# All experts computed in one dense loop over pairs of key and value chunks, in place of gathering each token's rows

## The reference

```python
def peer(h, w_query, sub_keys, expert_u, expert_v):     # h: 256 x 1024
    q = (h @ w_query).reshape(B, S, PEER_HEADS, 2, PEER_HALF)
    sc = jnp.einsum('bshcd,hckd->bshck', q, sub_keys)    # 8 heads, 2 halves, 128 keys
    sv, si = lax.top_k(sc, PEER_TOPK)                    # 16 of 128, twice a head
    cand_s = (sv[..., 0, :, None] + sv[..., 1, None, :]).reshape(B, S, PEER_HEADS, n_cand)
    cand_i = (si[..., 0, :, None] * N_KEYS + si[..., 1, None, :]).reshape(B, S, PEER_HEADS, n_cand)
    top_s, top_j = lax.top_k(cand_s, PEER_TOPK)          # 16 of 256 a head
    eidx = jnp.take_along_axis(cand_i, top_j, axis=-1)   # 128 experts a token, out of 16384
    gate = jax.nn.softmax(top_s, axis=-1)
    ...
        u, v = expert_u[et], expert_v[et]                # tables of 16384 x 1024
        act = jax.nn.gelu(jnp.einsum('tnd,td->tn', u, xt)) * gt
        return jnp.einsum('tn,tnd->td', act, v)
```

## Time and profile before

| | |
|---|---|
| median of 2 runs | 1561.11 us (1559.96 to 1562.26) |
| span of the profiled execution | 1554.9 us, first to last instruction |
| PE busy | 1212.9 us (78%) |
| DVE busy | 926.5 us (60%) |
| ACT busy | 431.5 us (28%) |
| POOL busy | 347.1 us (22%) |
| moved by DMA | 409.73 MB, of which 297.35 MB by POOL's queue |

### The profile page before, as it was taken

One profiled execution on the slowest core, in us unless ns is written; L12 is line 12 of the kernel. 1 busy time (PEld: TensorE's weight loads), 2 busy tenths in 40 slices (PEclk: granted clock), 3 DMA queues, 4 the chain that ended last, 5 costly groups with the idle time before them and its releaser, 6 DMA issues.

```text
span 1554.9 us, 26679 instructions
## 1 busy us (share of the span) xinstructions
PE 1212.9 (78%) x11282; PEld 834.9 (54%) x11282; DVE 926.5 (60%) x2067; ACT 431.5 (28%) x1094; POOL 347.1 (22%) x315
## 2 busy tenths in 40 slices
PE   7989898894385533457856775799987888999998
PEld 6467784772153100125524452468877774888843
DVE  2887666657797988785677655321455343455512
ACT  2111420132432422543364332423243211110100
POOL 1000012034354555454455544000000000000000
PEclk9997999996597855569878996899999999999999
DMA  9551459699999999999999999624300023344432
GB/s 381 195 191 66 144 205 390 238 383 419 414 410 420 420 422 421 421 414 419 416 421 420 420 418 418 240 82 163 109 9 3 4 111 108 122 163 161 137 140 104
DMA packets 109720, 409.73 MB, mean 264 GB/s; under 512 B 8456, under 2 KB 33552, under 8 KB 76448
## 3 DMA queue, kind: packets, MB, share of 16 engines
q0 software_dynamic: 44576, 297.35, 46.5%
q1 hardware_dynamic: 63552, 106.48, 19.2%
q10 hardware_dynamic: 1472, 4.20, 1.0%
HBM read 405.89 MB, written 2.11 MB: 262 GB/s over the span
## 4 chain that ended last, share of the span: by engine, by line
PE 58%; DMA 22%; DVE 10%; ACT 4%; issue 3%; POOL 2%; another core or an unknown queue 0%; POOLq 0%; DVEq 0%; ACTq 0%; SPq 0%
PE psum L502 20%; DMA arena<-in_experts,arena 17%; PE psum L1942 8%; PE psum L2454 5%; PE psum L512 4%; DVE arena L1490 4%; PE psum L1521 3%; DMA arena<-in_lora_up 2%; PE psum L755 2%; PE psum L1269 2%; POOL arena L1475 2%; PE psum L2244 2%; PE psum L760 2%; DMA arena<-in_ada_wT 2%; PE psum L741 2%
## 5 line engine op out<-in xcount | busy, mean ns | idle before, releaser
L1475 POOL DMA_INDIRECT arena<-in_experts,arena x256 | 317.1, 1239 | 383.2 <-PE psum L1521 299.8
L1521 PE MATMUL psum<-arena 128*32 128x512 f32 x1024 | 185.4, 805 | 238.2 <-ACT arena L1506 231.6
L502 PE MATMUL psum<-actT,weights 128*128 128x256 f32 x1312 | 287.3, 381 | 0.0
L502 PEld LDWEIGHTS psum<-actT,weights 128*128 128x128 f32 x1312 | 250.3, 191 | 35.7 <-issue 1.5
L1521 PEld LDWEIGHTS psum<-arena 128*32 128x32 f32 x1024 | 22.7, 121 | 329.5 <-ACT arena L1506 307.3
L1490 DVE CUSTOM_DVE_ANT_0 arena<-arena 128x1024 f32<-128x1024 f32 x96 | 116.7, 1224 | 50.9 <-DMA arena<-in_experts,arena 50.1
L1490 DVE CUSTOM_DVE_ANT_0 arena<-weights,arena 128x1024 f32<-128x1024 f32 x96 | 116.6, 1223 | 37.1 <-DMA arena<-in_experts,arena 35.1
L1496 ACT ACTIVATE arena<-arena 128x2 f32<-128x2 f32 x128 | 26.1, 204 | 364.3 <-DVE arena L1490 350.4
L1942 PE MATMUL psum<-arena 64*64 64x64 f32 (+1 forms) x2816 | 89.7, 231 | 17.4 <-DVE arena L2059 7.1
L1942 PEld LDWEIGHTS psum<-arena 64*64 64x64 f32 x2816 | 84.1, 142 | 26.0 <-issue 14.6
L1490 DVE CUSTOM_DVE_ANT_0 arena<-normed,arena 128x1024 f32<-128x1024 f32 x64 | 77.2, 1225 | 22.1 <-DMA arena<-in_experts,arena 20.3
(11 more groups left out here) (390 smaller groups left out, 1897.0 us busy)
## 6 DMA issues: line engine op xcount, KB each, us to landing
weights<-in_w_in SPq DMA_DIRECT2D x18, 2048.0 KB
arena<-in_ada_wT POOLq DMA_DIRECT2D x48, 512.0 KB, 6.3
weights<-in_ffn_w_up SPq DMA_DIRECT2D x22, 1024.0 KB
weights<-in_ffn_w_down SPq DMA_DIRECT2D x5, 2048.0 KB
weights<-in_w_out SPq DMA_DIRECT2D x4, 2048.0 KB
weights<-in_w_peer_q SPq DMA_DIRECT2D x4, 2048.0 KB
arena<-in_experts,arena POOLq DMA_INDIRECT x256
weights<-in_w_ple_gate SPq DMA_DIRECT2D x2, 2048.0 KB
```

What stands on the lines that cost most here:

```text
L502: mm = nc.tensor.matmul(out[:, c * T:(c + 1) * T], w[:, k, c * P:(c + 1) * P], act[:, k, :], start=(k == 0), stop=(k == kc - 1))
L1475: nc.gpsimd.indirect_dma_start(out=rows[:, n % RING, :], out_offset=None, in_=dram["experts"], in_offset=bass.IndirectOffsetOnAxis(ap=eidx ...
L1521: mm = nc.tensor.matmul(SUMS[sum_part(k, i), i, :], diag[:, pos, :], rows[:, pos, D + 512 * i:D + 512 * (i + 1)], start=first, stop=last, ...
```

## The change

The gather goes. The kernel now gets the two tables as `expert_u`, 128 chunks of 128 experts with the width on partitions, and `expert_v`, 128 chunks of 128 experts on partitions, 512 KB each, and computes all 16384 experts for all 256 tokens.

- `pe_queries` runs all four query tiles with their scores, and also the context's turning (`pe_ctx_chunks`, products with a diagonal that holds the norm) and its three tiles `ctx_v`, `ctx_lora`, `ctx_k` (in this order; `ctx_k` reuses the slot of `ctx_v`). All stays float32.
- A stage of DVE alone runs the first two of the eight selection turns, then comes the "beside" stage. It has 128 turns without any backbone: in turns 0 to 62 the 63 pieces of the context's scan with the 90 pieces of the other six selection turns spread over them (a scan piece first in each turn), and from turn 64 on the one-hots. `dve_scan_common`, the first piece on DVE, waits for the copy of `ctx_k`.
- The one-hots turn the list of (expert, gate) of each token into dense gates: for each token DVE builds a 128x128 one-hot of the high part of the numbers times the gate (L1483) and one of the low part (L1485, four tokens at once), PE multiplies the two (L1462) and ACT copies the result to `gsel` (L1498), 64 groups of four tokens. `pe_onehots` waits for the scan's end and all gates; the dense loop waits for the last copy.
- The dense loop has 64 pairs of chunks: 16 matmuls of 128x128 by 256 columns (keys of two chunks times tokens, L1118), one gelu of 128x512 on ACT (L1126), two products with `gsel` on DVE (L1148), 8 matmuls of 128x128 by 512 columns (values, L1166). PE takes the keys of the next pair ahead of the values of this one. SP loads the chunks into eight slots of the ring (`sp_experts`); the first eight need only the ring to be free.
- The ple projection (8 matmuls of 512 columns) now stands at the head of `pe_ple`, behind the loop; its inputs come by POOL's queue during the loop. The two gate broadcasts (16 matmuls of 128 columns) stand inside the loop.

```diff
+        def keys_at(pair):
+            return 4 * pair - 2 if pair else 0
+        def values_at(pair):
+            return 4 * pair + (4 if pair < PAIRS - 1 else 2)
...
+        def sp_experts(sp, first, last):
+            for s in range(first, last):
+                if s >= U_SLOTS:
+                    sp.wait_ge(S("exp_used"), s - U_SLOTS + 1)
...
+                sp.dma_start(ring_chunk(s), src).then_inc(S(f"exp_in{s % U_SLOTS}"), 16)
...
+        def pe_keys_of(pe, pair):
+            if pair >= 2:
+                pe.wait_ge(S("gelu_ok"), pair - 1)
+            for c in range(2):
+                w = pe_chunk(pe, keys_at(pair) + c).rearrange("p (k n) -> p k n", k=DC)
+                for k in range(DC):
+                    mm = nc.tensor.matmul(dots_bank(pair)[:, c * T:(c + 1) * T], w[:, k, :], actT[:, k, :],
+                                          start=(k == 0), stop=(k == DC - 1))
+                mm.then_inc(S("exp_used"), 1)
...
+            pe.wait_ge(S("gates_cp"), T // OH)
+            pe_keys_of(pe, 0)
+            for at in range(PAIRS):
+                if at + 1 < PAIRS:
+                    pe_keys_of(pe, at + 1)
+                w = [pe_chunk(pe, values_at(at) + c) for c in range(2)]
+                for b in (1, 0) if at + 1 < PAIRS else (0, 1):
+                    pe.wait_ge(S("weighted_ok"), TB * at + 2 - b if at + 1 < PAIRS else TB * PAIRS)
+                    for c in range(2):
+                        mm = sums(at, c, b, w[c])
...
+        def dve_onehots(dve, st):
...
+            for g in range(T // OH):
+                if g >= 2:
+                    dve.wait_ge(S("onehot_pe"), g - 1)
+                t = slice(OH * g, OH * (g + 1))
+                for k in range(OH):
+                    at = OH * g + k
+                    nc.vector.tensor_scalar(onehots[:, g % 2, 0, k, :], K("iota"), sel_i[:, at:at + 1], sel_g[:, at:at + 1],
+                                            ALU.is_equal, ALU.mult)
+                nc.vector.tensor_tensor(onehots[:, g % 2, 1], K("iota").unsqueeze(1).to_broadcast([P, OH, P]),
+                                        bc(sel_j[:, t], P, OH, P), ALU.is_equal).then_inc(S("onehot_ok"), 1)
...
-        def pool_rows(pool):
...
-                nc.gpsimd.indirect_dma_start(
-                    out=rows[:, n % RING, :], out_offset=None, in_=dram["experts"],
-                    in_offset=bass.IndirectOffsetOnAxis(ap=eidx[:, b, i:i + 1], axis=0),
-                ).then_inc(S(f"row{n % RING}"), 16)
...
+        SCAN_END = 64
+        turn = 0
+        for f in scan_stages(ctx_m, "c"):
+            spread(f, turn, turn + f["pieces"])
+            turn += f["pieces"]
...
+        spread(dict(act=lambda act: act_select(act, FIRST), dve=lambda dve, st: dve_select_rest(dve, st, FIRST),
+                    pieces=select_pieces(FIRST)), 0, SCAN_END - 1)
+        spread(dict(pe=pe_onehots, act=act_onehots, dve=dve_onehots, pieces=T // OH + 3), SCAN_END, NK - 2)
```

More of the change, by code:

```diff
@@ L170, in weight_tiles @@
     w = dram["w_in_2"]
-    tile("ctx_k", part(w, 0, DC, K20, 512))
     tile("ctx_v", part(w, 0, DC, V20, 512))
     tile("ctx_lora", part(w, 0, DC, LORA0, 128), width=128)
-    for i in range(2):
-        tile(f"ple_proj{i}", part(dram["w_ple_proj"], 0, 2, 512 * i, 512))
+    tile("ctx_k", part(w, 0, DC, K20, 512))
     for i in range(2):
@@ new lines, in act_values_of, with score_bank, ctx_bank @@
+        def act_values_of(act):
+            for pair in range(PAIRS):
+                act_gelu(act, pair)
+                if GATEBC_AT < pair <= GATEBC_AT + 2:
+                    g = pair - GATEBC_AT - 1
+                    act.wait_ge(S("gatebc_pe"), g + 1)
+                    nc.scalar.copy(gatebc[:, g, :], G[1]).then_inc(S("gatebc_ok"), 1)
+        def score_bank(b):
+            return aux[2 + b]
+        def ctx_bank(c):
+            free = G[tile_at["ctx_v"] % 2]
+            return (aux[0], aux[1], free[:, 0:512], free[:, 512:1024])[c % 4][:, 0:T]
@@ L1370, in dve_select @@
             scores = sc[b][:, 2 * heads[0]:2 * heads[-1] + 2, :]
-            turn = QUARTERS * b + quarter
+            es = slice(heads[0] * PK, (heads[-1] + 1) * PK)
+            tsc = gate[:, b, es].rearrange("p (h k) -> p h k", h=n_h)
+            eif = experts[:, b, es]
             dve.wait_ge(S("sc_cp"), TB * quarter + b + 1)
@@ L1418, in dve_select @@
             st.settle()
+            yield
             for h in range(n_h):
@@ L2655, in build, with spread @@
-        n_groups = TB * GROUPS
-        pieces[GROUPS + 4].append((len(beside), 0))
-        beside.append(dict(act=act_ple_load, pieces=1))
-        pieces[-1].append((len(beside), 0))
-        beside.append(dict(act=act_block0_squares, pieces=1))
-        assert len(pieces) < n_groups, len(pieces)
+        FIRST = 2
+        stage(dve=lambda dve, st: dve_select_first(dve, st, FIRST))
+        beside = []
+        pieces = [[] for _ in range(NK)]
+        def spread(f, begin, end):
+            n = f["pieces"]
+            for k in range(n):
+                pieces[begin + k * (end - begin) // n].append((len(beside), k))
+            beside.append(f)
```

837 lines of the change are left out of this document (308 added, 529 removed).

## The result

The changed kernel takes 2175.9 us (median of 2171.96 and 2179.87) against 1561.1 us: a ratio of 1.396, 95% interval 1.390 to 1.401. That is slower by 615 us; the forecast was 2179 us, 618 slower. The profiled execution is that of 2179.87 us, with a span of 2178.0 us.

The account below looks back on a forecast made before the run. The prediction took the gather's transfers to bound the kernel before. Its terms 391 + 210 + 108 + 896 + 4.5 + 563.1 gave a span of 2172.6 us; with 6.2 us to the median, 2179 us, range 2125 to 2240.

Parts of the forecast that it names:

- The dense loop: 64 pairs of chunks at 13.94 us of PE each, loads hidden, plus 4 us of gate broadcasts: 896 us.
- The queries' stage: Query tiles, scores and context tiles on PE until the copy of `ctx_k`: ends at 391 us.
- Scan and six turns: Context scan with six selection turns, a chain longer than DVE's own work: 210 us, between 160 and 258.
- The upper bound: Scan stage with no selection piece hidden: 164 us of chain plus 94 of selection, 258 us.
- The one-hots: 64 groups of four tokens at 1.6 us, plus 6 us at the ends: 108 us, between 93 and 122.
- the row's value and the rule: One-hots: profile row's PE clock of 0.82 gives 108 us; the skill's rule of a high clock gives 99.
- Behind the loop: Projection and a copy ahead of the norm's transposes add 4.5 us; all else stays 563.1 us.
- (a): Scan stage: selection doesn't fit between the rungs, 258 us instead of 210, time 2227 us; chance 10%.
- (b): Dense loop: PE doesn't keep the full clock; at 0.82 it takes 197 us more, 2376 us; chance 5%.
- (c): Dense loop: a PE record is a whole matmul, so a pair costs 6.97 us, time 1733 us; chance 3%.
- (d): Dense loop bound by its transfers, 5.0 us a pair, 320 us instead of 892, time 1607 us; chance 1%.
- (e): Scan stage runs at DVE's floor of 160 us, time 2129 us; counted within the forecast's 80%.

Follow-up runs that it names:

- Run 4: The kernel before with rows of 4 KB: only the key half of each row gathered and also read by the sums, half the bytes; 1454.7 us.
- Run 1: The changed kernel with each value product of the dense loop taken over 256 of its 512 columns; 1957.5 us.
- run 2: The changed kernel loading only the left half of each chunk, half the loop's bytes, with all products kept; 2175.6 us.
- run 3: The changed kernel with the dense loop's operands in bf16, chunks cast by loads over POOL's queue; 1620.75 us, 1.039 of the kernel before.
- run 8: The changed kernel with the four one-hot TENSOR_SCALARs of each group done twice on DVE; 2246.9 us.
- run 9: The changed kernel with dense loop and one-hots in bf16 and five selection turns ahead of the scan; 1585.2 us, 1.018 of the kernel before.
- run 10: As run 9, with gates and gelu results in bf16 and 40 pairs' key products between the one-hot groups; 1493.5 us, 0.958 of the kernel before.
- run 7: The changed kernel with two of the four one-hot TENSOR_SCALARs of each group left out; 2152.1 us.

## Why the prediction was right, point by point

**The bound of the kernel before**: right. Run 4 shows it, and shows its depth: after 103 us something else comes last, with DVE the fullest. The slices at 9 reach from 311 to 972 us, not 330 to 990 as I had read them, which changes no term.

**The dense loop**: right in mechanism and size. Forecast 896 us, measured 885.2 (720.2 to 1605.4); a pair takes 13.83 us for 13.94, since blocks follow each other 6.9 us apart where a single tile was read as 6.99, and this holds the gate broadcasts too. Run 1 shows that columns set it, run 2 that bytes don't, run 3 that the data type does. The DMA share was 0.46, not the 0.36 that 134 MB at the gather's 420 GB/s would give: these loads of 512 KB kept the queues busier by the byte, which cost nothing.

**The queries' stage**: 394.5 us for 391. DVE stood idle 45.4 us before L1679, as forecast (347 to 391; measured 349 to 394). The 3.5 us come from ahead of the stage: the first scores begin at 302.38 us, 3.85 later than before.

**Scan and six turns**: 217 us for 210. Directions were right (70.3 us for 72); the pairs came to 122 for 112, mainly because my 25 us for a bare pair were PE's busy time in rows 10, and a bare pair takes 26.9 us. The upper bound's base of 164 us was too low, 180.2 measured: 7.6 us for the same reason, and 10 because its sum (4 x 25 + 2 x 24 + 16) leaves out the chain at the end. With the right base the bound would have been 274, and the 217 lie well below either. Against the table's 220.5, which has the transposes for the one-hots in it, the 210 lack 7.6 us in the four bare pairs, 2.5 in the pieces beside them and 3.2 at the end, and have 2.8 too many elsewhere.

**The one-hots**: 108.9 us for 108, and the agreement is luck, for two terms were wrong and cancel. I had DVE at 1.45 us a group and lifted it to 1.6 with a clock of 0.82. The clock was 1.00 behind the first groups, so the lift is gone; of the row's value and the rule, I chose the wrong one. DVE itself takes 1.63 us, since its TENSOR_SCALARs begin 0.26 us apart, not 0.21 as MAX8 does ((1.11 - 0.33)/3 = 0.26); the last operation holds 0.60 us of the group, as forecast. Of the two signs that I gave, DVE over 85% busy if the clock holds and PE near 100% if it doesn't, the first came: 105.9 of 109 us. PE's own price was too low at both levels, 1.16 us a group for 1.01 and, in run 8, 2.07 for 1.9.

**Behind the loop**: the 4.5 us of the projection came as forecast (8.1 us for 3.5 ahead of the transposes). The rest was 4.8 us longer than in the profile of before (564.5 us from the transposes on, for 559.7), less than the 7.9 us by which two executions of this kernel differ. Of it 2.6 us lie in one stretch behind the chain of the scan over tokens, 21.1 us for 18.4 with the same 281 records of PE: the granted clock was 0.92 there and 1.00 before. For the remainder I have no cause.

**The sum**: 2172.6 us of span forecast, 2178.0 measured: +3.5, +7, +1, -11, +5. The 6.2 us added for the way from this profile's span to the median were wrong for the new kernel: its median is 2.1 us below its profiled span. A time is 1.9 us above its own span (2179.87 for 2178.0), and the rest is how far one execution lies from another. 5.4 us too few and 8.3 too many leave 3: an agreement closer than the terms deserve.

**The rivals**: (a) the selection doesn't fit between the rungs: partly true, 40 of its 94 us are in the open, where the 2227 us had all of them there. (b) and (c) are out: the clock was 1.00 through 885 us, and run 3 shows one record a product only for bf16. (d) wanted PE about three times as fast; in f32 it wasn't, and in run 3, where it is, the loop goes at its bytes. (e) is out: DVE was busy 158 us of 217, as its floor of 160 said, and the chain is longer.

## What to carry to other kernels

A gather of few rows and a dense pass over all of them are compared by two prices, bytes for the one and passes of PE for the other; halved bytes are no gain where the dense pass is in f32. When a stage that ran under long transfers is taken away, add up what it hid and where the new long stage can cover anything: here the loop of 885 us covered nothing. In f32 the 270 us without transfers ahead of it cost nothing, since PE sets the loop; in bf16, where the transfers do, putting products that need no gates there took 92 us off. A piece of other work on an engine that works in order is free only where nobody waits for that engine: between the rungs most of it was, in the directions hardly any.

## What the runs showed of the hardware that I had not expected

- DVE took 319 ns (run 9) for a TENSOR_SCALAR of 128x128 from and to bf16, with two per-partition operands in f32, and 333 ns in f32; a TENSOR_TENSOR of 128x512 with both inputs broadcast took 695 and 674 ns. The weighting product of 128x256, whose inputs are packed, did gain in run 10, 288 ns for 422. The Trainium skill (VectorE: DVE Perf Modes, Rules for kernel authors) names four times for copies and scalar operations and twice for TENSOR_TENSOR, with dense bf16 in SBUF. The broadcast inputs aren't dense, and the packed product gained 1.5 times; for the TENSOR_SCALARs, at this size of 128 elements a partition, the trace shows nothing of it. What part of their 319 ns is a fixed cost, no run here separates.
- Loads that cast f32 to bf16 over POOL's queue (run 3) read 2.10 MB in 5.01 us, 419 GB/s, as fast as the gather's plain rows at 420.
- With rows of 4 KB (run 4) the stage moved 253 GB/s at a DMA share of 0.77, with rows of 8 KB 415 at a share of 1.01.
- PE's clock was 0.50 at the start of the one-hot stage in the changed kernel and in runs 7 to 10. It rose to 1.00 where PE then worked without a pause (6.75 us in the changed kernel, 6.6 in run 7, 13 in run 10), and stayed at 0.50 through all the groups where PE paused in each from the first on (0.70 us in run 8, 0.89 us in run 9).
